# Second mixer of a two-block transformer: ScalarE rounds the first two query chunks ahead of its copies of the joined key product

## The reference, cut to what matters

```python
w = ev_w_in[j]                 # 1024 x 1992, split by columns:
# 0:512     queries of the latent attention        ("qa")
# 512:640   latent c_kv                            ("ckv")
# 640:1152  indexer queries, 8 heads of 64         ("qi")
# 1152:1224 indexer key (64) and head weights (8)  ("ki", "wi")
# 1224:1736 queries of the window attention        ("qb")
# 1736:1992 its keys and values                    ("kb", "vb")
```

## Time and profile before

| | |
|---|---|
| time, median of 3 runs | 2263.3 us (2257.35 to 2263.88) |
| profiled execution, its own time | 2258.24 us |
| its span | 2256.4 us |
| mean granted clock of TensorE, as a share of full speed | 0.971 |
| busy: PE, DVE, ACT, POOL | 94%, 69%, 57%, 9% of the span |
| at the place of the change: ACT's token copies end at | 637.12 us |
| PE's joined product ends at | 640.82 us |
| PE's first matmul of qi starts at | 645.82 us |

### The profile page before, as it was taken

How to read it: one execution, slowest core, us unless ns; L and a number is a source line. 1 busy time by engine, 2 the same in 40 slices (tenths; PEclk the granted TensorE clock), 3 DMA queues, 4 the chain that set the end, 5 groups by cost and what they waited for, 6 DMA issues and landing times. The chain is left out here.

```text
span 2256.4 us, 32624 instructions
## 1 busy us (share of the span) xinstructions
PE 2125.9 (94%) x11988; PEld 1708.2 (76%) x11988; DVE 1552.7 (69%) x2214; ACT 1275.9 (57%) x1681; POOL 198.1 (9%) x148
## 2 busy tenths in 40 slices
PE   8997999998988989998998899999999999999996
PEld 8986884443777778997768688888888888888885
DVE  4557651221555676665477889888888888888887
ACT  4555441111334554443464777787777878777784
POOL 2112100000000104340001010101000010101000
PEclk9999998999987999999899899999999999999998
DMA  8640649999552244558312899999999999999994
GB/s 259 190 161 1 196 163 376 416 416 415 186 177 94 85 150 149 191 182 197 105 39 86 305 375 366 372 372 371 370 371 374 372 376 371 375 367 375 368 396 171
DMA packets 293950, 602.53 MB, mean 267 GB/s; under 512 B 17835, under 2 KB 123711, under 8 KB 285520
## 3 DMA queue, kind: packets, MB, share of 16 engines
q1 hardware_dynamic: 285392, 571.56, 70.0%
q0 software_dynamic: 8448, 29.49, 4.1%
HBM read 595.15 MB, written 5.83 MB: 266 GB/s over the span
## 5 line engine op out<-in xcount | busy, mean ns | idle before, releaser
L2167 ACT ACTIVATE arena_rounded<-ring 128x1024 fp32r<-128x1024 f32 x452 | 471.2, 1061 | 114.8 <-DMA ring<-in_moe_w_up_dram 65.5
L2884 DVE TENSOR_TENSOR ring_rounded<-ring,arena_rounded 128x1024 fp32r<-128x1024 f32 x452 | 525.8, 1220 | 11.9 <-ACT arena_rounded L2167 9.3
L1221 PE MATMUL psF<-arena_rounded 128*128 128x512 f32 x896 | 357.6, 399 | 1.6 <-ACT arena_rounded L2189 1.6
L1223 PE MATMUL psF<-arena_rounded 128*128 128x512 f32 x896 | 354.3, 395 | 0.0
L1222 PE MATMUL psF<-ring_rounded,arena_rounded 128*128 128x512 f32 x896 | 352.9, 394 | 0.0
L2441 DVE TENSOR_TENSOR ring_rounded<-ring,ring_rounded 128x2048 fp32r<-128x2048 f32 (+1 forms) x68 | 147.1, 2165 | 166.8 <-ACT ring_rounded L1982 166.5
L1223 PEld LDWEIGHTS psF<-arena_rounded 128*128 128x128 f32 x896 | 168.5, 188 | 39.2
L1221 PEld LDWEIGHTS psF<-arena_rounded 128*128 128x128 f32 x896 | 168.8, 188 | 38.8 <-ACT arena_rounded L2189 1.8
L1222 PEld LDWEIGHTS psF<-ring_rounded,arena_rounded 128*128 128x128 f32 x896 | 168.7, 188 | 37.8
L1222 PE MATMUL psB<-ring_rounded,PT_rounded 128*128 128x512 f32 x448 | 177.7, 397 | 0.0
L1982 ACT ACTIVATE ring_rounded<-ring 128x2048 fp32r<-128x2048 f32 (+1 forms) x71 | 128.5, 1814 | 82.2 <-PE psF L1223 62.7
(11 more groups left out here) (490 smaller groups left out, 4632.1 us busy)
## 6 DMA issues: line engine op xcount, KB each, us to landing
ring<-in_moe_w_gate_dram SPq DMA_DIRECT2D x224, 512.0 KB, 5.7
ring<-in_moe_w_up_dram SPq DMA_DIRECT2D x224, 512.0 KB, 5.5
ring<-in_moe_w_down_dram SPq DMA_DIRECT2D x224, 512.0 KB, 5.4
ring<-in_w_dram SPq DMA_DIRECT2D x48, 1024.0 KB, 16.3
arena<-in_w_dram SPq DMA_DIRECT2D x16, 1024.0 KB, 19.0
ring<-in_w_in_dram SPq DMA_DIRECT2D x14, 1024.0 KB, 5.4
ring<-in_ff_w_gate_dram SPq DMA_DIRECT2D x11, 1024.0 KB, 7.2
ring<-in_ff_w_up_dram SPq DMA_DIRECT2D x11, 1024.0 KB, 9.7
```

The source lines that it names most:

```text
L1221: mm(bank, x1, w1, start=start, stop=False, skip_group_check=open_groups)
L1223: return mm(bank, x2, w1, start=False, stop=stop, skip_group_check=open_groups)
L2167: ap_(half_slot(slot, w_hi).bitcast(R32), half_slot(slot, raw_halves), ACT.Copy).then_inc(q["high"], 1)
L2884: V.tensor_tensor(half_slot(slot, low_halves).bitcast(R32), half_slot(slot, raw_halves), half_slot(slot, w_hi), ALU.subtract).then_inc(q[" ...
```

## The change

ACT's list is changed in one place. Before, it copies the joined product out (`save_unit(first)`) and then rounds the two qi chunks (`weight_highs(...)`); now it rounds first and copies then. No instruction is added, removed or given another size, and no other engine's list changes.

```diff
@@ -2336,8 +2336,8 @@
                 save(f"ln{3 * i + 3} transposed")
                 if i == 0:
                     first, end = span("mix2")
+                    weight_highs(last_chunk("mem2 keys and values"))
                     save_unit(first)
-                    weight_highs(last_chunk("mem2 keys and values"))
                     for u in range(first, end):
                         if u > first:
                             save_unit(u)
```

## The result

The changed kernel takes 2244.13 us (median of 6 runs, 2240.07 to 2250.14), the kernel before 2262.45 us (6 runs, 2253.53 to 2264.44). The ratio, from kernels run side by side, is 0.993, with a 95% interval of 0.9907 to 0.9953: faster, clear of noise though by under 1%, and worth about 15.8 us. (The two medians lie 18.3 us apart; the ratio and its interval are the measure.) The prediction was 2257.6 us, a gain of 5.7 us, most likely within 0.3%, and a range that ended at 2250.

What follows compares the result with a forecast made beforehand. It took the stretch to be bounded by the chain rounding, low part, PE, whose head stood behind unneeded copies. Wait 4.35 plus clock 1.33 gave 5.7 us off 2263.3, so 2257.6 us; range 2250 to 2264.

Steps and rivals of the forecast that it cites:

- The release and the wait: At PE's first qi matmul: PE waits for the first low part, so roundings moved ahead start it 4.35 us earlier.
- The clock term: First qi product: with a pause of only 0.65 us PE keeps full clock, gaining 1.33 us, from 0 to 1.73.
- Only the wait goes: Rival at the first qi chunk: the gain is 4.35 us without any clock gain, giving 2258.9 us; chance 0.18.
- the release is not the low part: Rival at PE's qi start: something else releases PE, gain 0, time stays 2263.3 us; chance 0.09.
- The copies behind the roundings: ACT's three joined-product copies: roundings fit the 3.74 us of idle time before them; cost 0, at most 0.1 us.
- From there ACT, DVE and PE hand over to each other as before: Behind the third rounding: no other engine comes to the front, and weight loads move along with the products that release them.
- the sum: Whole kernel: 4.35 us of wait plus 1.33 us of clock, 5.68 us, said as 5.7 us.
- a later slow spell changes, for the better: Rival in this mixer's attention: its slow spell vanishes, up to 10.1 us more gain, 2247.5 us; chance 0.15.
- The rule that the prediction weighed against its clock term: Clock monitor runs freely, so the clock rises at different points each run; gain 4.35 plus a draw from 0 to 1.73 us.
- The base: Whole kernel: forecast starts from 2263.3 us, median of three runs, 5.1 us above the profiled execution.

## Why the prediction was wrong

*The release and the wait: right.* Predicted 4.35 us, measured 12.45 − 7.98 = 4.47; the rest of 0.12 is that the first rounding starts at 633.49, 0.14 us before the row of the token copies ends (629.88 + 3.75), where the prediction had it start at that end. The pause was to be 0.65 us and is 0.52. The low part is what PE waits for; the kernel that rounds twice shows it. One rounding ahead gives the same, so of the two moved only the first did anything.

*The clock term: right in the first trace, but its bound was too low.* Predicted 1.33 us. From the first qi matmul to the copy of its result it is now 643.88 − 637.86 = 6.02 us instead of 7.38, a gain of 1.36. In the third trace of the kernel before the lower clock held for 6.9 us and not 3.4, from an earlier point of the pause on,

```profile
641.90:648.80 6.90, 6.17 (x29) 6.21 (x30) 6.87 (x6) 0.10 (x1) 0.00 (x0) 0.51 0.06 19
```

and the stretch was 1.3 us longer (13.55 against 12.22). Against that execution the change is worth 2.7 us here, beyond the 1.73 that the prediction gave as the most. "Only the wait goes" (4.35) is refuted, and so is "the release is not the low part".

*The copies behind the roundings: right,* at nothing. They start at once, with no one waiting.

*The step that failed* is the sentence "From there ACT, DVE and PE hand over to each other as before", and with it the sum, which ended at 700 us. The order of the handovers is as before, but the speed of PE in them isn't a constant of the kernel. With the work moved up by some 6 us at the place of the change, the attention has 10.2 us at the lower clock instead of 23.9, and the third mixer loses one spell of 6.8 in the first trace and has other spells in the two repeats. Together with the 0.7 us ahead of the attention that is 6.6 us, more than the local gain. I had this as a rival ("a later slow spell changes, for the better"), with 0.15, and set the floor of the range, 2250, where 7.6 us of its 10.1 would still be inside (three quarters of the bound; the prediction's words, "three quarters of half its bound", misstate its own sum). The windows of the earlier trace rows were right to be read; the chance was too small. What stood in the trace for it: the spell is long (24 us), begins after a pause of PE, and lies in a stretch where PE is busy only 79%.

*The size of that rival was off too.* I bounded the attention's spell at 10.1 us for 25, or 0.40 us for each us at the lower clock. It was 3.5 us for 13.7 less, or 0.26: PE has idle time there that takes up a part of it, and the busy times of ACT and DVE are the same at either clock (34.3 and 34.2, 32.1 and 32.2 us in the windows above). In the third mixer it is 3.4 us for 6.8, or 0.49, between the first traces of the two kernels, in a spell through which PE is busy all the time:

```profile
706.95:730.80 23.85, 19.55 (x76) 13.27 (x77) 11.78 (x57) 14.92 (x52) 0.00 (x0) 0.50 0.08 28
...
1099.50:1106.20 6.70, 6.70 (x20) 5.53 (x20) 4.63 (x13) 0.60 (x1) 0.00 (x0) 0.50 0.23 81
```

These are two slow spells of the kernel before: in the first PE has idle time to slow down into, in the second it has none. In the other two traces of the changed kernel both spells of 6.8 us in the third mixer are gone and one of 10.2 stands further back, with PE idle for a part of it:

```profile
1099.10:1109.50 10.40, 9.96 (x49) 6.01 (x49) 6.54 (x40) 6.62 (x27) 0.00 (x0) 0.51 0.00 1
```

There the mixer took 126.85 us, 3.8 less than before with only 3.4 us less of the lower clock. So it matters where a spell lies as well as how long it is, and 0.49 is the figure of one pair of traces, not a price of that stretch. The bound was too high for the one stretch, and the other had not been looked at; I had listed the third mixer only from 1112 us on.

The rule that the prediction weighed against its clock term fits in half. The kernel before does see one fall of its clock at different points, from trace to trace (13.55 against 12.22 us). But the attention came at 58.36, 58.36 and 57.84 us before and 54.86, 54.81 and 54.90 after: what the shift did to the attention was the same each time. The Trainium skill ("TensorE: Matmul & The Clock Gate", section "Part 1: The HAM clock gate") also advises to model the ramp as less than 1% of a typical kernel's span; here an edit of 1.95 us moved 0.5% of the span through it, the size of the whole question.

*The base was high too.* The sum starts from 2263.3 us, the median of three runs. Larger samples of the kernel before have medians of 2260.45 (23 runs) and 2258.9 (29 runs). From the lower of them the forecast would have been 2253.2, still 9 us above the measured 2244.13, so this isn't the step that failed.

*What stays open.* That the surplus belongs to the edit and comes without the pause is shown for the attention: 8 matmuls ahead of the joined product bring the long spell back with no pause, and the kernels with 18 matmuls and with the roundings done twice give the same later stretches for the same shift. Which moment each stretch needs, and what ties it to the place of the change and not to the start of the execution, isn't something that these runs tell. The third mixer's part of the surplus (2.6 us in the mean) is less sure than the attention's, since the kernel before had that stretch in 127.43 us once, without any edit. One rival is thinned but not excluded: added matmuls shift the work and also keep PE busy, and only the kernel that rounds twice shifts it without adding any. Nor is the last line of the table of stretches (1.5 us) pinned down; it differs by 4.8 us between traces of the changed kernel alone. And the kernel with 12 matmuls has its ratio without the attention that was to give it, and without any other stretch of its traces that would.

## What to carry to other kernels

A rounding that is ready goes ahead of a copy that must still wait, on an engine that works in order: look for idle time on it in front of an instruction that waits, with ready work behind. Where a later stretch has PE partly idle and spells of a low granted clock, a local gain of x us is not a forecast of x: add the price of each such spell to both sides of the range, by the time it would cost on that stretch's own path (here 0.26 us for each us at the lower clock in the attention, and 0.49 for one spell in which PE was busy throughout). And the way to test whether a surplus is the edit's own is to keep the edit and add a little work in front of it.

## What the runs showed of the hardware

- A small delay can cost several times its size: 8 matmuls ahead of the joined product, 1.95 us by themselves, took the ratio from 0.9935 to 0.9986, some 11.5 us. With 12 of them it was 0.9951, in the medians alone; the traces with 8 and with 12 take the same time from there on.
- The same shift gave the same later stretches by a pause (5.24 us) and by work without one (5.33 us): 58.3 us in both attentions, 128.97 in both third mixers.
- A fall of the clock cost less where PE had idle time: 13.7 us less of it gave 3.5 us in the attention, and one spell of 6.8 us less, with PE busy all through it, gave 3.4 in the third mixer (one pair of traces).
- A shorter pause ahead of the attention (0.74 instead of 2.53 us) went with 3.4 us at the lower clock instead of 10.2, at the same work, and with 3.5 us less in all, of which 1.8 are the pause itself.
- Without any edit the kernel before had its third mixer in 130.65, 130.67 and 127.43 us, and the stretch from the first rounding to the one at 620 took 605.1 to 616.0 us in sixteen traces of kernels whose code is the same there.
